# Splitting sixteen gather rows as six and ten in a two-layer diffusion block with expert retrieval

## What is computed

```python
def chunk(xc):                                  # 128 tokens
    ...
    idx = e1 * PEER_NKEYS + e2                  # (128, 8 heads, 16)
    g = jax.nn.softmax(sv, axis=-1)
    u = u_tab[idx]
    a = jax.nn.gelu(jnp.einsum('chkd,cd->chk', u, xc), approximate=False)
    w = (g * a).astype(xc.dtype)
    return jnp.einsum('chk,chkd->cd', w, v_tab[idx])
```

## Time and profile before

| | |
|---|---|
| median of 3 runs | 2797.2 us (2792.89 to 2809.17) |
| the profiled execution's own time | 2789.94 us |
| its span in the trace | 2787.9 us |
| first layer's gathers issued | 228.5 to 1818 us |
| second layer's gathers issued | 2023 to 2769.1 us |
| gathers | 1536, 805.40 MB |
| DVE busy | 1533.0 us (55%) |
| PE busy | 1475.0 us (53%) |
| POOL busy | 1472.4 us (53%) |
| traffic over the span | 333 GB/s |

### The profile page before, as it was taken

The page is one execution under the profiler, slowest core; times in us unless marked ns, Lnnn a source line. Parts: engine busy times, 40 slices in busy tenths (PEclk is TensorE's granted clock), DMA queues, the critical chain, the costliest instruction groups (busy, mean ns, idle before and its releaser), DMA issues.

```text
span 2787.9 us, 23279 instructions
## 1 busy us (share of the span) xinstructions
PE 1475.0 (53%) x7838; PEld 762.5 (27%) x7838; DVE 1533.0 (55%) x3968; ACT 337.9 (12%) x660; POOL 1472.4 (53%) x1546
## 2 busy tenths in 40 slices
PE   7896754546566665455434533367853333333243
PEld 4675531123334332122101210045741100000000
DVE  1328668668654746555665554325366665466442
ACT  1311110112201110110001000024110000000000
POOL 0004667665665556554666666600056666666664
PEclk8998986767777775567555765689986566665655
DMA  9718999998999999999999999930389999999997
GB/s 320 247 61 289 374 399 402 347 354 299 366 389 367 343 350 397 394 395 393 399 371 372 397 395 377 352 126 31 106 321 382 367 361 362 368 352 371 356 379 289
DMA packets 338901, 928.61 MB, mean 333 GB/s; under 512 B 27600, under 2 KB 141024, under 8 KB 338528
## 3 DMA queue, kind: packets, MB, share of 16 engines
q0 software_dynamic: 221184, 805.40, 75.6%
q1 hardware_dynamic: 117600, 121.73, 13.2%
HBM read 925.98 MB, written 1.05 MB: 333 GB/s over the span
## 4 chain that ended last, share of the span: by engine, by line
DMA 20%; PE 19%; DVE 19%; POOL 18%; issue 12%; another core or an unknown queue 9%; ACT 2%; SPq 1%; POOLq 0%; DVEq 0%; ACTq 0%
POOL RING L628 18%; DMA RING<-in_p_v,IDV 10%; DMA RING<-in_p_u,IDX 8%; DVE RING L711 7%; PE acc L1176 5%; PE wk L1238 2%; PE wk L1372 2%; DMA WR<-in_ada_w 2%; PE wk L1358 2%; PE wk L1162 2%; DVE TI L700 1%; PE wk L1318 1%; DVE TV L697 1%; DVE OHR L961 1%
## 5 line engine op out<-in xcount | busy, mean ns | idle before, releaser
L711 DVE SCALAR_TENSOR_TENSOR RING<-RING,acc 128x1024 f32<-128x1024 f32 x768 | 915.4, 1219 | 615.2 <-DMA RING<-in_p_u,IDX 475.6
L1176 PE MATMUL acc<-RING,ST 128*32 128x512 f32 x3072 | 633.1, 951 | 945.8 <-DMA RING<-in_p_v,IDV 756.2
L628 POOL DMA_INDIRECT RING<-in_p_u,IDX x768 | 734.4, 956 | 725.2 <-DVE WG L972 426.6
L628 POOL DMA_INDIRECT RING<-in_p_v,IDV x768 | 736.4, 959 | 571.7 <-PE acc L1176 233.9
L1176 PEld LDWEIGHTS acc<-RING,ST 128*32 128x32 f32 x3072 | 123.3, 148 | 1348.7 <-issue 1328.5
L1372 PE MATMUL wk<-HT,WR 128*128 128x256 f32 x768 | 176.3, 390 | 1.3 <-ACT HT L1036 1.3
L1372 PEld LDWEIGHTS wk<-HT,WR 128*128 128x128 f32 x768 | 149.9, 197 | 33.9 <-issue 11.6
L1404 PE MATMUL wk<-SELW,WE 128*128 128x512 f32 x96 | 80.3, 931 | 102.1 <-DVE WE L732 94.9
L1238 PE MATMUL wk<-WR,HT 128*128 128x256 f32 x512 | 120.8, 391 | 10.6 <-issue 8.6
L1238 PEld LDWEIGHTS wk<-WR,HT 128*128 128x128 f32 x512 | 98.6, 196 | 37.7 <-issue 23.3
L1135 ACT ACTIVATE GA<-A 128x16 f32<-128x16 f32 x48 | 10.3, 216 | 783.6 <-DVE RING L711 451.0
(11 more groups left out here) (177 smaller groups left out, 1608.3 us busy)
## 6 DMA issues: line engine op xcount, KB each, us to landing
WR<-in_ada_w SPq DMA_DIRECT2D x31, 1024.0 KB
WR<-in_p_w_q SPq DMA_DIRECT2D x24, 1024.0 KB
RING<-in_ada_w SPq DMA_DIRECT2D x17, 1024.0 KB, 12.1
WR<-in_o_w_in SPq DMA_DIRECT2D x14, 1024.0 KB
RING<-in_p_u,IDX POOLq DMA_INDIRECT x768
RING<-in_p_v,IDV POOLq DMA_INDIRECT x768
WR<-in_e_w_in SPq DMA_DIRECT2D x8, 1024.0 KB
WR<-in_e_w_out SPq DMA_DIRECT2D x7, 1024.0 KB
```

The lines of the kernel that those rows point to most:

```text
L628: pool.indirect_dma_start(out=ring[:, n % NU, :], out_offset=None, in_=tables[table], in_offset=bass.IndirectOffsetOnAxis(ap=rows, axis=0) ...
L711: nc.vector.scalar_tensor_tensor(out=U[:, s % NU, :], in0=U[:, s % NU, :], scalar=1.0, in1=acc[:, 1, :], op0=ALU.mult, op1=ALU.mult, accum ...
L1176: ins = nc.tensor.matmul(acc[32 * g:32 * g + 32, 0, hf * 512:hf * 512 + 512], ST[:, c % 2, s, :], V[:, s % NV, hf * 512:hf * 512 + 512], s ...
```

## The change

The split of the 16 rows becomes 6 for u and 10 for v, and since 16 is a multiple of neither, the place in a ring is counted over the whole run (n = 16c + s) instead of within a chunk. The same rule is used by the gather, by the dot and by the matmul, and the count awaited for a slot's landing becomes n // NU + 1 or n // NV + 1 transfers.

```diff
-NU = NV = 8
+NU, NV = 6, 10
...
             def gather_u(c, s):
-                if c > 0 or s >= NU:
-                    pool.wait_ge(dotted, c * TOPK + s - NU + 1)
+                n = c * TOPK + s
+                if n >= NU:
+                    pool.wait_ge(dotted, n - NU + 1)
                 col = (c % PH) * TOPK + s
-                gather("u", U, s, IDX[:, (c // PH) % 2, col:col + 1], u_in)
+                gather("u", U[:, n % NU, :], IDX[:, (c // PH) % 2, col:col + 1], u_in[n % NU])
...
             def gather_v(c, s):
-                if c > 0 or s >= NV:
-                    pool.wait_ge(vsum, c * TOPK + s - NV + 1)
+                n = c * TOPK + s
+                if n >= NV:
+                    pool.wait_ge(vsum, n - NV + 1)
...
                 for s in range(4 * q, 4 * q + 4):
-                    dve.wait_ge(u_in[s % NU], 16 * (2 * c + s // NU + 1))
-                    nc.vector.scalar_tensor_tensor(out=U[:, s % NU, :], in0=U[:, s % NU, :], scalar=1.0,
+                    n = c * TOPK + s
+                    dve.wait_ge(u_in[n % NU], 16 * (n // NU + 1))
+                    nc.vector.scalar_tensor_tensor(out=U[:, n % NU, :], in0=U[:, n % NU, :], scalar=1.0,
...
-                for s in range(4 * q, 4 * q + 4):
-                    pe.wait_ge(v_in[s % NV], 16 * (2 * c + s // NV + 1))
+                first = c * TOPK + 4 * q
+                for m in range(first, first + 4):
+                    pe.wait_ge(v_in[m % NV], 16 * (m // NV + 1))
...
-                                               V[:, s % NV, hf * 512:hf * 512 + 512],
+                                               V[:, (first + g) % NV, hf * 512:hf * 512 + 512],
```

## The result

The changed kernel took 2848.6 us (median of 5 runs, 2834.2 to 2851.5), the kernel before, run between them, 2797.8 us (5 runs, 2792.9 to 2809.2). The ratio is 1.0153, with an interval of 1.0130 to 1.0175: **slower by 1.5%, some 43 us**, where I had forecast +0.5% and a range that ended at 2843. (The two medians lie 51 us apart; I go by the ratio throughout.) The profiled execution was the fastest of the five, 2834.2 us with a span of 2832.2 us, against 2789.9 and 2787.9 before: +44 us.

The account below looks back on a forecast made before the run. The prediction saw nearly full DMA engines in the gather stages, POOL only 5% faster than its transfers, and the v ring tight. Terms -21 - 19 + 56 = +16 us gave 2806 us profiled, 2812 us as median; range 2772 to 2843 us.

Parts of the forecast that it names:

- The margins, the exchange of waits: POOL's gathers: margins 6.8 (u) and 6.9 us (v); v idle from 342 to under 120, u idle from 69 to 230-330.
- The v term: Gathers waiting for v rows: ten rows let POOL issue 28 gathers between pauses, not some 20; -21 us, 0 to -60.
- Starts and ends of layers: First and last v gathers of each layer wait less with two more rows: -19 us, bounds -8 and -25.
- The u term: Gathers waiting for late dots to free one of six u rows, holding v gathers back too: +56 us, +20 to +80.
- last item: In the u wait estimate: POOL arrives earlier without its v wait, so u waits lengthen, +12 us.
- overhangs of dots: Dots ending after the u gather six behind was issued: 24 places, 133 us, less today's 69 us of u waits.
- the choices' double parts: Stretches where two parts of a choice follow each other: the largest growth should be there; no size given.
- Clearly slower: Rival: DVE's own updates are held too, a later pause loses time again and u gathers wait; 2837 us, chance 0.16.
- No change: Rival: in the gather stages one wait takes the other's place, u overhangs half hidden; -5 us, 2792 us, chance 0.26.
- "faster" rival: Late updates unrelated to POOL's pauses, so v waits outside full stretches go; -34 us, 2763 us, chance 0.18.

Follow-up runs that it names:

- r_6_8: Six u rows and eight v rows (two ring rows empty) against the kernel before with 8 and 8, timely updates: 1.0016, +4 us.
- t_6_8: Six u rows and eight v rows (two rows less in all) against the kernel before with 8 and 8, late updates: 1.0090, +25 us.

## Why the prediction was right in its direction and wrong in its size

**The margins, the exchange of waits.** Right. v 8 and v 520 no longer wait (0.30 us); v idle fell to 127 us (I had said under 120), u idle rose to 321 (230 to 330). But v 10 and v 522 did not wait either (0.30 us; I had said 2 to 3). 1070 to 1380 us stayed as it was (189 gathers for 184).

**The v term, -21 us.** Near enough as long as eight u rows stand beside: -29 us (+-10) for ten v rows against eight, with the starts and ends of layers in it, for which I had -40 in sum. Its reason held in part: from 2050 to 2780 us POOL paused for over 1 us 22 times (35 before), after up to 41 gathers on end (28 before), and mostly for 4 to 5 us (2 to 3.5 before). But the pauses did not all move out: 15, 24 and 33 gathers on end take turns. These are two neighbouring pauses of the changed kernel there, the first behind 33 gathers, the second behind 15:

```profile
2222.55 0.94 POOL L628 DMA_INDIRECT RING<-in_p_v,IDV  x1 [4.08 <-remote]
...
2245.66 0.94 POOL L628 DMA_INDIRECT RING<-in_p_u,IDX  x1 [4.78 <-DVE RING L714]
```

**Starts and ends of layers, -19 us.** The starts were not won. v 10 was issued at 288.05 (293.17 before), but in this trace the first gather of all was already 6.0 us earlier (222.55 for 228.51), so counted from there v 10 came 0.9 us later. The u waits that the prediction itself lists (u 10 now waits 5.98 us) took the gain: two chunks into either layer the changed kernel stood within 1 us of where it stood at the layer's first gather. I had added a gain on the v side in a place where the next wait was already on the u side. The ends came about as worked out: from the last u gather of the first layer to its last v gather it is 23.9 us for 28.9, in the second layer 24.0 for 29.6, some 10 us in all where I had 9.

**The u term, +56 us.** This is the step that failed. With the v rows' -29 the measured +43 leaves +72 us for taking two u rows beside ten v rows; beside eight they cost +25. So the halves alone were not dearer than I had them (+25 for +44, which is the u term without its last item; -29 for -40). What I had too small is that last item, +12 for "POOL arrives there earlier without its v wait": the runs put what the two rings do to each other at +47 us (+-16). I had counted the overhangs of dots in the trace of before, 133 us in 24 places, as if the dots would come when they came then. The overhangs did not say where u waits would grow. Counted again, they come to 124 us in 23 places, of which 6 us lie from 1070 to 1380 us and 2 us from there to the layer's end; u idle beyond the 0.30 rose by 54 us in each of these two stretches. (Some 18 us, not 40, of the overhangs lie in slices of the earlier trace rows with 389 GB/s or more, where the forecast had them hidden by a full queue.) From 420 to 1070 us it rose by 99 us, where the overhangs make 51. There, as I read it, the dots' times were themselves a product of POOL's v pauses: between 639 and 702 us before, POOL stopped every 8 gathers. The changed kernel ran on for 16, an update for the attention came 15.7 us after TensorE's end instead of at once, and POOL, which had not waited for that dot before, waited 12 us for it. The stretch from 420 to 1070 us lost 37 us. That same step named the choices' double parts as the places of growth. The second layer, where they stand without any attention, lost next to nothing. And I had held a gather's own time fixed: it grew from 956 and 959 to 965 and 968 ns, 13 us in all, which the forecast named as a sign against it. Why, no run shows.

The split of the miss: -40 forecast for v with the starts and ends, -29 measured, 11 us; +56 forecast for u, +72 left over, 16 us. That these make up the 27 us between +16 and +43 is no check, since the +72 is the rest. (All this takes the cost of the missing weight slot as the same with 8 and 10 v rows, and the intervals of the terms are 6 to 16 us wide either way.)

**The rivals.** "Clearly slower" (DVE's own updates are held too, and a later pause costs it again; 2837 us) is nearest to what happened, with one correction: in the place shown the updates held were TensorE's, ScalarE and VectorE waited for them, and POOL for VectorE. I gave it 0.16, on the evidence of one wait of 5.04 us in the earlier trace rows. "No change" fell with late updates: the waits did take each other's place almost one for one (-215, +252), but not place by place: from 420 to 1070 us u idle rose by 99 us and v idle fell by only 70. The "faster" rival's condition, v waits that have nothing to do with POOL's pauses, is met where updates are timely, and there the change is faster, by 10 us rather than 34. Had the comparison been made there, the forecast would have missed in direction too: that it had the sign right owes something to luck. The Trainium skill's fit (DMA: Bandwidth & Descriptors, Anatomy of one DMA, SWDGE (gpsimd) path) gives an estimate of 3.2 us for a gather, where the earlier trace rows has 6.84 us; by that estimate six u rows would have had ample margin. With timely updates they nearly had (`r_6_8`, +4 us), with late ones not (`t_6_8`, +25 us).

**Open.** What holds the updates back, and why it does so in some sets of runs and not in others. What makes the 23 us that the two rings cost each other with timely updates. Whether a pause of 3 us or more set on purpose would deliver them: it was not tried. How much of the +72 us is the held attention and how much the shorter u ring alone was read from one trace, not measured apart.

Of the kernels run that compute everything, the one with 8 u and 10 v rows and two slots of weights had the lowest ratio in both conditions (0.9906 and 0.9978; with late updates that is no clear lead). It pays for the v rows with a slot of weights, which alone costs 13 and 23 us.

## What to carry to other kernels

Waits on one queue of instructions are not independent: a pause that looks like loss may be what keeps another engine on time, so the times at which the other ring's rows come free can't be read from the trace of before once the pauses are moved. When rows are shifted between two rings, price each side alone and both together; here -29 and +25 made +43. And where a kernel's time differs by some 6% between sets of runs, a change of 1% can have either sign: run both kernels under both conditions before believing it.

## What the runs showed of the hardware

- In some sets of runs semaphore updates reached their waiters several us late while GpSimd issued gathers, 15.7 us in the place shown. Of the 370 that came over 1.5 us late in the kernel before, 323 were TensorE's, 47 VectorE's and none ScalarE's. The one shown came 3.1 us after GpSimd had stopped (670.16); 258 of the 370 fall into its pauses of over 1 us, the other 112 do not. The kernel before takes 2798 to 2804 us with this and 2643 us without, 155 to 161 us less.
- Half the bytes in each gather did not take the lateness away (444 gathers for 451 in 650 us of the second layer, a pause mostly after 23 to 25).
- The queue's pace is 1.24 to 1.25 us per gather of 128 rows whether a row has 2 or 4 KB; 0.94 us of it is the instruction.
